# Expert gate table by accumulating single-word transfers, low parts of the up tiles on VectorE, up sums over eight PSUM banks

## The reference

```
def run(hc):
    q = (hc @ w_query).reshape(chunk, 8, 256)                 # 8 heads
    s1 = einsum('thd,nd->thn', q[..., :128], k1)              # 128 scores
    s2 = einsum('thd,nd->thn', q[..., 128:], k2)              # 128 scores
    v1, i1 = top_k(s1, 16);  v2, i2 = top_k(s2, 16)
    cand = v1[..., :, None] + v2[..., None, :]                # 16 x 16
    sc, pos = top_k(cand, 16)                                 # 16 picks
    eidx = take(i1 * 128 + i2, pos)                           # of 16384 experts
    g = softmax(sc)
    a = einsum('thkd,td->thk', expert_u[eidx], hc)
    act = gelu(a) * g
    return einsum('thk,thkd->td', act, expert_v[eidx])
```

## Time and profile before

| | us |
|---|---|
| median of 3 runs | 3030.32 |
| lowest, highest | 3025.0, 3035.52 |
| span of the profiled execution | 3005.5 |

### The profile page before, as it was taken

One profiled execution on the slowest core, in us unless ns is written; L12 is line 12 of the kernel. 1 busy time (PEld: TensorE's weight loads), 2 busy tenths in 40 slices (PEclk: granted clock), 3 DMA queues, 4 the chain that ended last, 5 costly groups with the idle time before them and its releaser, 6 DMA issues.

```text
span 3005.5 us, 40609 instructions
## 1 busy us (share of the span) xinstructions
PE 2977.4 (99%) x15170; PEld 2562.3 (85%) x15170; DVE 1692.1 (56%) x2918; ACT 1269.3 (42%) x2109; POOL 1450.7 (48%) x747
## 2 busy tenths in 40 slices
PE   9999999999999999999999999999999999999998
PEld 7887888888888888899999997778888889888887
DVE  5826359998999701068888875363121436631223
ACT  6555344335777633333333334353233334532332
POOL 6731443444444444577878503644444443444442
PEclk9999999999999999999999999999999999999999
DMA  4242332444677765599999953213333322123332
GB/s 147 93 139 79 105 101 85 136 141 135 181 209 201 211 195 168 189 327 371 361 377 360 375 192 117 80 64 98 94 96 98 110 70 71 49 92 98 98 98 85
DMA packets 331163, 473.18 MB, mean 157 GB/s; under 512 B 125764, under 2 KB 235236, under 8 KB 330488
## 3 DMA queue, kind: packets, MB, share of 16 engines
q1 hardware_dynamic: 308472, 403.79, 41.8%
q0 software_dynamic: 22528, 67.19, 6.0%
HBM read 405.97 MB, written 60.86 MB: 155 GB/s over the span
## 4 chain that ended last, share of the span: by engine, by line
PE 95%; issue 1%; DVE 1%; POOL 1%; DMA 1%; ACT 0%; SPq 0%; DVEq 0%; POOLq 0%; ACTq 0%
PE pb L893 29%; PE pb L894 29%; PE pb L895 29%; PE pb L1223 2%; PE pb L1516 1%; PE pb L1074 1%; POOL s_over L753 0%; PE pb L1173 0%; PE pb L1102 0%; PE pb L1357 0%; PE pb L1377 0%; PE pb L1041 0%; PE pb L941 0%; PE pb L1278 0%; DMA s_ring<-ev 0%
## 5 line engine op out<-in xcount | busy, mean ns | idle before, releaser
L753 POOL TENSOR_TENSOR s_over<-s_ring,s_rhigh 128x1024 fp32r<-128x1024 f32 x401 | 999.6, 2495 | 1362.4 <-ACT s_rhigh L1624 1361.7
L1624 ACT ACTIVATE s_rhigh<-s_ring 128x1024 fp32r<-128x1024 f32 x525 | 555.3, 1059 | 1086.4 <-DMA s_ring<-w 498.6
L893 PE MATMUL pb<-s_over,s_rhigh 128*128 128x512 f32 (+1 forms) x2392 | 876.7, 367 | 0.9 <-DVE s_over L2471 0.8
L895 PE MATMUL pb<-s_over,s_over 128*128 128x512 f32 (+1 forms) x2392 | 872.8, 365 | 0.0
L894 PE MATMUL pb<-s_over,s_rhigh 128*128 128x512 f32 (+1 forms) x2392 | 872.7, 365 | 0.0
L893 PE MATMUL pb<-s_hS,s_rhigh 128*128 128x512 f32 (+1 forms) x1664 | 649.8, 390 | 3.6 <-DVE s_hS L2782 2.5
L895 PE MATMUL pb<-s_hS,s_over 128*128 128x512 f32 (+1 forms) x1672 | 645.0, 386 | 0.0
L894 PE MATMUL pb<-s_hS,s_rhigh 128*128 128x512 f32 (+1 forms) x1664 | 641.7, 386 | 0.0
L893 PEld LDWEIGHTS pb<-s_over,s_rhigh 128*128 128x128 f32 x2392 | 449.1, 188 | 56.0 <-issue 1.3
L895 PEld LDWEIGHTS pb<-s_over,s_over 128*128 128x128 f32 x2392 | 449.0, 188 | 53.2
L894 PEld LDWEIGHTS pb<-s_over,s_rhigh 128*128 128x128 f32 x2392 | 449.1, 188 | 52.9 <-issue 1.0
(11 more groups left out here) (310 smaller groups left out, 3166.9 us busy)
## 6 DMA issues: line engine op xcount, KB each, us to landing
s_ring<-w SPq DMA_DIRECT2D x272, 512.0 KB, 3.5
s_ring<-eu SPq DMA_DIRECT2D x128, 512.0 KB, 4.0
s_ring<-ev SPq DMA_DIRECT2D x128, 512.0 KB, 6.2
acts<-s_arena SPq DMA_DIRECT2D x128, 256.0 KB, 4.0
s_arena<-acts SPq DMA_DIRECT2D x128, 192.0 KB, 5.2
s_arena<-gates SPq DMA_DIRECT2D x128, 192.0 KB, 6.6
gates<-s_arena SPq DMA_DIRECT2D x36, 512.0 KB, 5.0
gates<-s_arena SPq DMA_DIRECT2D x6, 1024.0 KB, 7.5
```

The lines of the kernel that those rows point to most:

```text
L753: gp.tensor_tensor(rlow[:, s, :, :], ring[:, s, :, :], rhigh[:, s, :, :].bitcast(F32), ALU.subtract).then_inc(S("w_split"), 1)
L893: mm(dst, a_high, b_high, start=start, stop=False)
L895: return mm(dst, a_low, b_high, start=False, stop=stop)
L1624: sc.activation(rhigh[:, s, :, :], ring[:, s, :, :], ACT.Copy).then_inc(S("w_high"), 1)
```

## The change

The table is no longer computed on TensorE. It is set to zero early, by 24 DMAs of 1 MB from a small tile of zeros (`zero`), one behind each of 24 weight loads of the gate and output stages. VectorE computes, inside each head's round, the softmax of that head's gates (`gate_scale`, with ScalarE's `gate_exp`) and the word addresses of its picks (`g_at`). GpSimd then puts the gates of the first 384 tokens into the table with 8 x 3 x 16 = 384 indirect DMAs of 128 single words each, with `compute_op=ALU.add`, so that a word that two heads picked gets both. A head's DMAs for a block of 128 tokens wait until those of the head before for that block have landed (`g_put0` to `g_put2`).

GpSimd no longer makes low parts from U tile 2 on; VectorE does, up to eight per head between the pieces of its round (`low_beside`), the rest behind it. The 12 transposes, the 384 products, the one-hots and the copies are gone, and so are SP's 42 stores. U sums rotate over all eight banks. SP waits behind the last U load for all 384 DMAs (`g_put0` to `g_put2`), then loads the first four pairs of `act_in`; pairs 4 to 7 follow one by one behind the first four V loads.

```diff
@@ block.sync
-            tiles(T_GATE + RING, T_QUERY + RING, T_GATE + RING)
+            sp.wait_ge(S("zeroed"), 1)
+            for q in range(ZQ):
+                tile(T_GATE + RING + q, a["w"][T_GATE + RING + q])
+                sp.dma_start(gzero[q], zero[:, :].unsqueeze(1).to_broadcast([P, NK * NK * TD // (ZQ * P * ZW), ZW]))\
+                    .then_inc(S("table_zero"), 16)
...
-                if part < 7 and 0 <= b < TD // GB:
-
-                    i0, i1 = G_PART[part:part + 2]
-                    sp.wait_ge(S("gb_copied"), (b + 1) * (GB // 4))
-                    sp.dma_start(gtab[i0:i1, :, b * GB:(b + 1) * GB].rearrange("n p t -> p n t"), gbuf[:, b % 2, i0:i1, :])\
...
+            for t in range(TT - 1):
+                sp.wait_ge(S(f"g_put{t}"), 16 * PH * TOPK)
+            for e in range(4):
+                sp.wait_ge(S(f"a_out{e}"), 32)
+                act_in(e, e)
@@ block.gpsimd
-            splits(T_QUERY, T_U + 120)
+            splits(T_QUERY, U_LOW)
+
+            gp.wait_ge(S("table_zero"), 16 * ZQ)
+            for h in range(PH):
+                gp.wait_ge(S("gate_done"), h + 1)
+                for t in range(TT - 1):
+                    if h >= 1:
+
+                        gp.wait_ge(S(f"g_put{t}"), 16 * TOPK * h)
+                    for k in range(TOPK):
+                        n = h * TOPK + k
+                        gp.indirect_dma_start(gate1, bass.IndirectOffsetOnAxis(ap=g_at[:, t, n:n + 1], axis=0),
+                                              score[:, t, h, k:k + 1], None, compute_op=ALU.add)\
+                            .then_inc(S(f"g_put{t}"), 16)
@@ block.tensor
-                if t % 8 == 0:
-                    pe.wait_ge(S("oh2_done"), t // 8 + 1)
-                pe.wait_ge(S("oh_low"), t + 1)
-                mm(pb[:, 4 + (t // 2) % 4, (t % 2) * 2 * P:(t % 2 + 1) * 2 * P], oh2[t // 8 % 2][:, t % 8, :],
-                   oh1[:, t % 16, :, :].rearrange("p e i -> p (e i)"), start=True, stop=True).then_inc(S("oh_used"), 1)
-                if t % 8 == 7:
-                    up(T_U + U_TOP + t // 8, U_TOP + t // 8)
-            for k in range(U_REST, NK):
-                up(T_U + k, k)
+            for k in range(NK):
+                if k == 4:
+                    pe.wait_ge(S("s_copied"), PH)
+                up(T_U + k, k, banks=8)
@@ block.scalar
+                h, r = divmod(k - LOWS_1 + LOWS, LOWS)
+                if r == 0 and h < PH:
+                    gate_exp(h)
+                if k >= 125:
+                    for e in ((0, 1), (2, 3), (4, 5, 6, 7))[k - 125]:
+                        gated_high(e)
@@ block.vector
+            def gate_scale(h):
+
+                ve.wait_ge(S("gate_exp"), h + 1)
+                g = gneg[:, h % 2, :, :]
+                ve.tensor_reduce(gsum, g, AX.X, ALU.add).then_inc(S("gate_sum"), 1)
...
+                ve.tensor_tensor(score[:, :, h, :], g, gsum.unsqueeze(2).to_broadcast([P, TT, 16]), ALU.mult)\
+                    .then_inc(S("gate_done"), 1)
...
+                low_beside(i, 3)
+                if i >= 1:
+                    gate_scale(i - 1)
...
+            while lowered[0] < T_V:
+                low_next()
             for k in range(8):
                 gated(k)
                 if k >= 1:
                     gated_low(k - 1)
+                if k % 2:
+                    low_next()
```

More of the change, by code:

```diff
@@ L98 @@
 T_END = T_F1 + 64
-U_TOP = 36
-U_GATE = TD // 8
-U_REST = U_TOP + U_GATE
+U_LOW = T_U + 2
+LOWS_1, LOWS = 4, 8
 W_QKNA, W_QKD = 0, 8
@@ L412, in program @@
         rows = a["ev"].rearrange("n e c o -> (n e) (c o)")
-        gtab = gates.rearrange("b n p t -> (b n p t)")[0:NK * NK * TD].rearrange("(n p t) -> n p t", p=NK, t=TD)
+        gflat = gates.rearrange("b n p t -> (b n p t)")[0:NK * NK * TD]
+        gtab = gflat.rearrange("(n p t) -> n p t", p=NK, t=TD)
+        gate1 = gflat.rearrange("(n one) -> n one", one=1)
+        gzero = gflat.rearrange("(q p n c) -> q p n c", q=ZQ, p=P, c=ZW)
         actS = Area().take(2, 2, 8, T, dt=F32R)
@@ L435, in program @@
         pabf = C.take(2, 64)
-        choice = C.take(2, TT, P)
+        choice = C.take(2, TT, 16)
         score = C.take(TT, PH, TOPK)
[L438 to L446, removed]
+        gsum = C.take(TT)
+        chosen = C.take(TT, P)
+        g_at = C.take(TT - 1, P, dt=U32)
+        g_atf = C.take(TT - 1, 16)
+        gneg = C.take(2, TT, 16)
+        tok = C.take(TT)
         s_row = C.take(P, dt=U32)
@@ L449, in program @@
         s_act = C.take(P)
-        s_tok = C.take(1)
+        at_ch = ARENA - 2 * DC * T
+        assert C.at <= at_ch
         s_mul = score[:, TT - 1, :, :].rearrange("p h k -> p (h k)")
@@ L689, in _ @@
                 act_out(124 + r)
+                sp.wait_ge(S("e_raw"), r + 1)
+                act_in(4 + r, 4 + r)
             for e in range(4):
@@ L818, in pick_act @@
                     .then_inc(S(f"s_act{j // 16 % 2}"), 16)
-            gp.wait_ge(S("gate_sum"), 13)
-            for e in range(2):
-                gp.wait_ge(S(f"gates_out{e}"), 7 * 8 * (TD // GB))
+            gp.wait_ge(S("s_listed"), 4)
             for j in range(6):
                 fetch_row(j)
-            splits(T_U + 120, T_V + RING)
             for e in range(4):
@@ L1234, in expert @@
                 pe.wait_ge(S("e_act"), g * step + (k + 1))
-                for c in (4, 5, 6, 7, 0, 1, 2, 3):
-                    if k == 0 and c == 0 and not step:
+                for c in range(DC):
+                    if k == 0 and c == 4 and not step:
                         pe.wait_ge(S("e_read"), NK)
```

224 lines of the change are left out of this document (78 added, 146 removed).

## The result

The changed kernel takes 3047.36 us in the median of 5 runs (3039.74 to 3051.81), the kernel before 3033.52 in runs beside them: ratio 1.005, 95% interval 1.0032 to 1.0068. The forecast was 2981 us, faster. First the page of the changed kernel: span, busy shares, the chain that ended last.

The account below looks back on a forecast made before the run. TensorE, busy 99% of 3005.5 us, was taken as the bound: 3005.5 - 50.5 + 1.5 = 2956.5 us of span, plus the 24.8 us by which the runs' median exceeds the span, gives 2981 us; stated range 2970 to 3065.

Parts of the forecast that it names:

- rival 1: GpSimd's accumulating DMAs too slow, 1.73 or 2.24 us a turn; TensorE waits at first expert; 3161 us at 2.24; chance 0.24.
- The sign that it named for this failure: If accumulation is misjudged, TensorE idles once, for long, at the first expert, ended by GpSimd's DMAs, `act_in`, VectorE.
- What goes, 50.5 us: U stage on TensorE: without the table's work 746.8 us becomes 696.3, a gain of 50.5 us.
- Eight banks nothing: U stage: eight banks instead of four give nothing by themselves, as TensorE has no wait there to remove.
- Zeros, 0: Gate stage: 24 MB of zeros in 24 DMAs behind weight loads; price 0 to 10 us, taken as 0.
- Low parts on VectorE, 0: U stage: eight low parts per head make VectorE's round 38.6 to 42.3 us, under 43.5; cost taken as 0.
- Rival 2: U stage: VectorE becomes the bound, a head taking 44.3 to 48 us; 3002 us; chance 0.05.
- rival 3: U stage: the DMAs' single words crowd out the weights, waits of perhaps 15 us together; 2996 us; chance 0.05.
- 384 accumulating DMAs: GpSimd, U stage: at 1.4 us a turn they end at 1063 us, 142 us before the deadline; hidden up to 1.77.
- Disturbance by VectorE: VectorE's work stretching GpSimd's DMAs: gather turn 1.25 us undisturbed, 1.60 beside VectorE; 1.4 taken, both ends hidden.
- The start of the V stage, +1.5: V stage start: `act_in` loads between V loads bring SP to V tile 4 later; 1.5 us taken, some 6 above.
- The 24.8 us "outside the span": Amount by which the median of timed runs stands above the profiled span, added to 2956.5 us.

Follow-up runs that it names:

- run 9: Changed kernel with its up sums over four PSUM banks instead of eight, first expert behind all reads of them: 3044.55 us, one run.
- run 2: Changed kernel with the 384 DMAs writing their words instead of adding them: 3284.3 us, ratio 1.0849.
- run 3: Changed kernel without the last head's gates, 48 of the 384 DMAs: 2974.41 us, ratio 0.981.
- run 10: On top of run 8, GpSimd's 384 DMAs begun earlier (VectorE's low parts, first head's exponential and scaling earlier): 2991.4 us, ratio 0.9887.
- run 11: On top of run 10, the first head's 48 DMAs write instead of adding, a memset behind every second one: 2974.96 us, ratio 0.9839.
- run 4: Changed kernel with the first six row gathers moved behind the wait for the activations' stores: 3050.58 us, ratio 1.0055.
- run 8: Changed kernel, gathers spread and later, first V loads and last activation stores before SP's wait, V tiles 0 to 2 split earlier: 3013.46 us, ratio 0.9945.
- run 7: As run 2 (writing instead of adding), with a memset on GpSimd between every two DMAs: 2969.64 us, ratio 0.9806.
- run 5: Kernel before, with GpSimd's gathers at the start of the V stage spread, at most three per expert tile: 3017.23 us, ratio 0.9962.
- run 6: Changed kernel with the same spreading of the gathers at the start of the V stage: 3031.96 us, ratio 1.0009.
- run 1: Kernel before, once more with no edit: 3030.68 us, ratio 1.0.

## Why the prediction was wrong, point by point

The forecast was 2981 us and faster, with 0.74 on faster; measured were 3047 us and slower. The stated range, 2970 to 3065, holds the time, since it was drawn to take in rival 1 up to a turn of 1.98; the side was wrong. The sign that it named for this failure came: TensorE stands idle once, for long, at the first expert.

- **What goes, 50.5 us.** Right: the stage took 746.8 us and takes 696.4 (527.06 to 1223.5), 50.4 us less; 696.3 were foreseen. Eight banks nothing: right, shown by run 9.
- **Zeros, 0.** Right: 318 GB/s, DMA share 0.98, TensorE busy in all of 75 us; a DMA of zeros landed in 7.5 us.
- **Low parts on VectorE, 0.** Right. In the U stage VectorE waited 324.8 us in 96 places for ScalarE's rounding, TensorE for nothing. Rival 2 didn't come, nor rival 3: TensorE never missed a weight beside 384 x 128 added words.
- **384 accumulating DMAs: the step that failed.** Its frame held: start 519.4 foreseen, 519.5 found; edge 1.77 us a turn; 38.4 us for each 0.1 above. What failed is "I take 1.4" for a turn, read off the gather because it was the nearest row. It is 1.947: the bare turn is 1.85 and not 1.25, since the issue of an adding DMA takes 1.547 us and not 0.95, and the rest is VectorE's. By the step's own rule that is (1.947 - 1.77) x 384 = 68 us behind the edge, and TensorE waited 65.6; with 2981 it makes 3049 for 3047.4 measured. That this fits so closely is in part luck: a DMA was foreseen to land 6 us after its issue and the last one released SP 1.65 us after it, while SP's release had to come by 1203 and not 1205; the two nearly cancel. So it is rival 1 that came, between its 1.73 and 2.24, and its first figure, the issue growing with the ends of a word, was near: 1.547/0.95 = 1.63 times, not 1.5. I gave it 0.24 because "the issue of a gather need not scale with its words". The step had a gap of 0.37 us to its edge and no row of the operation; the value should not have come from a row of another kind. Runs 2, 3, 10 and 11 show the term from four sides: the addition's 0.585 us, 48 DMAs fewer, a start 26 us earlier, the first head's words written instead of added.
- **Disturbance by VectorE.** I had let it carry the whole uncertainty (1.25 to 1.60). It is (1.643 - 1.547) x 384 = 37 us, 0.10 us a turn where up to 0.35 were allowed for. Small beside the addition's 0.585, but not beside the wait: without it the turn would be 1.85, and by the step's own rule some 31 us of the 65.6 would be left (an estimate from these rows). In the trace of the changed kernel the 158 of these DMAs that no VectorE instruction overlaps are stretched over 1.546 us by 0.2 us together, the 97 that only a low part overlaps by 12.0, the 129 beside other VectorE work by 24.9. The Trainium skill's page "SBUF — State Buffer", section "SBUF: two separate sides", says that a VectorE instruction with two SBUF inputs contends with a GpSimd instruction that reads SBUF: the trace agrees in that the low parts, which have two inputs, stretch these DMAs, by 0.12 us each in the mean. Its figure of 3100 ns, which the prediction had weighed, is for a DMA beside a copy, and no DMA here reaches it: 2595 ns is the longest of 384.
- **The start of the V stage, +1.5.** The step counted landings within the stage, and that cost nothing: in run 3, without the long wait, TensorE waits 0.75 us at V tile 4, as before. What it didn't look at is the way from SP's release to the first expert, put at "about 10 to 12 us" in the deadline. It was 20.7: eight loads on SP ahead of the first V tile's, and six row gathers of 512 KB beside them. Runs 4 (7 us) and 8 (11 us) take it apart. Without the long wait it would not have shown: in run 3 there is none at the first expert.
- **The 24.8 us "outside the span".** Wrong: 1.8 us lie there. The profiled execution of the kernel before lacked the slow stretch that its timed runs have. The sum came out near all the same, and that is luck: the changed kernel has the stretch too, 24.0 us between the two V stages; run 3, with the wait gone, is at 2974 where the forecast was 2981.

What stays open is how GpSimd's issuing slows TensorE. Shown is that issuing less densely prevents it (run 7 against run 2) and that spreading mends more than half of it (5 and 6 against 1). Density alone doesn't settle when it begins: the 3005.5 us execution issued its first 31 gathers of the V stage at 1.41 us a turn and had no slow stretch, run 1 at 1.31 and had one; and from a burst's start to the first slow product it took between 8 us (run 1) and 47 us (run 2). It isn't the number of packets: from the page's rows of the software queue an adding DMA is 144 packets ((77824 - 70912)/48), a writing one 112 fewer ((77824 - 34816)/384), and the adding ones at 1.85 us a turn don't do it. Nor is it the clock: in run 1 TensorE was slow already at 1290 to 1299 us (29 products in 9 us) at a granted clock of 1.00. Nor is it full DMA engines: in run 1 they did next to nothing from 1312 to 1325, and the 3005.5 us execution had them full (a share of 1.04) at 1290 to 1299 and came through. Whether TensorE's instructions themselves reach it late was not tried: in run 1 the instruction queues moved nothing from 1299 to 1325, which fits a TensorE that needs few as well as one that waits for them. A slow stretch was seen only where these gathers or writes were issued densely; why one execution in several escapes it was not tried.

## What to carry to other kernels

When a step rests on an operation that no row shows, and the edge is nearer than the operation's possible cost, forecast by the edge: say on which side it falls with chances, and don't let the nearest row of another operation choose. Where several us of serial issue on one queue must end before a join, shorten the join's own chain too: weights and stores that don't need the result go ahead of the wait. And compare the profiled execution's time with the timed runs before trusting a difference between them to lie outside: here it was a stretch of the program that one execution lacked.

## What the runs showed of the hardware

- Where VectorE leaves it alone, an indirect DMA of 128 single words issues in 0.94 to 0.96 us from GpSimd whether it gathers or writes, and so does a gather of 128 rows of 4 KB (0.94 to 1.00); an accumulating one takes 1.547. The gap to the next is 0.30 in each.
- The recorded 1.547 us is the issue, not the addition in DRAM: the next starts 0.30 us after it, 384 times. The Trainium skill, "Perfetto Trace Analysis", section "DMA Instruction — SWDGE (GPSIMD)", says that the profiler's end of such a DMA is the end of making its descriptors and not of moving the data; the trace agrees, SP being released at 1268.65, 1.65 us after the last issue ended.
- GpSimd issuing gathers or plain writes back to back (1.25 to 1.27 us a turn where nothing stretches them) can slow TensorE to a product per 0.7 to 2.8 us, mostly 0.7, 1.4, 2.1 or 2.8 us apart in run 2. It set in 8 to 47 us into a burst and ended 3 to 10 us behind the burst's last DMA (runs 1 and 2). VectorE has less to do then, and its work was the only thing seen to stretch GpSimd's DMAs, so the state feeds itself until GpSimd pauses (run 1: from 1307 to 1320 us all of GpSimd's gathers took 0.94 to 0.95 us). That it feeds itself is my reading of the traces and no run of its own. At 1.64 us a turn (a memset of 0.33 us between) and with adding DMAs at 1.85 it didn't occur.
